# Nine weight slots instead of six in the expert loops of a hybrid decoder, with another gather and another layout of the second weight

## The reference, cut to what matters

```python
def layer(x):
    x = layer_norm(ALPHA * x + mixer(x))          # attention, then GDN in layer 1
    return layer_norm(ALPHA * x + moe_ffn(x))

def expert_block(args):                           # xb: the tokens of expert e
    xb, e = args
    hb = jax.nn.silu(xb @ w1[e]) * (xb @ w3[e])   # w1, w3: 1024 x 512
    return hb @ w2[e]                             # w2: 512 x 1024
```

## Time and profile before

| what | value |
|---|---|
| times of 3 runs | 1581.01, 1584.68, 1586.67 us (median 1584.68) |
| profiled execution: time, span | 1582.79 us, 1581.0 us |
| busy PE, PE weight load, DVE, ScalarE | 76%, 56%, 29%, 17% of the span |
| TensorE clock granted, mean | 0.934 |
| DMA over the whole span | 461.77 MB, 292 GB/s, 63246 packets |
| expert weights | 192 DMAs of 2 MB, median 26.5 us from issue to landing |

### The profile page before, as it was taken

How to read it: one execution, slowest core, us unless ns; L and a number is a source line. 1 busy time by engine, 2 the same in 40 slices (tenths; PEclk the granted TensorE clock), 3 DMA queues, 4 the chain that set the end, 5 groups by cost and what they waited for, 6 DMA issues and landing times. The chain is left out here.

```text
span 1581.0 us, 40565 instructions
## 1 busy us (share of the span) xinstructions
PE 1202.8 (76%) x17935; PEld 891.0 (56%) x17935; DVE 457.4 (29%) x1369; ACT 274.8 (17%) x676; POOL 34.8 (2%) x42
## 2 busy tenths in 40 slices
PE   8999676666666666799989899997866666666664
PEld 4444464554554554588888887543655555455553
DVE  1344511111111111465656544313211111111113
ACT  1232200000000000235244346202000000000000
POOL 0000300000000000000000000002000000000000
PEclk9999799999999999899999999998899999999998
DMA  9620599999999999943300001405799999999995
GB/s 362 243 107 16 196 425 426 427 425 426 429 425 426 428 426 423 355 160 107 129 32 1 1 28 55 157 4 236 313 427 426 425 427 427 426 425 428 425 427 234
DMA packets 63246, 461.77 MB, mean 292 GB/s; under 512 B 3872, under 2 KB 4016, under 8 KB 30416
## 3 DMA queue, kind: packets, MB, share of 16 engines
q1 hardware_dynamic: 61680, 455.90, 70.2%
q0 software_dynamic: 1504, 5.00, 0.9%
HBM read 459.83 MB, written 1.05 MB: 292 GB/s over the span
## 5 line engine op out<-in xcount | busy, mean ns | idle before, releaser
L711 PE MATMUL bank<-ring,arena 128*32 128x128 f32 x8192 | 311.0, 311 | 282.8 <-DMA ring<-in_moe_w 280.1
L711 PEld LDWEIGHTS bank<-ring,arena 128*32 128x32 f32 x8192 | 268.9, 123 | 332.9 <-DMA ring<-in_moe_w 241.3
L1009 ACT ACTIVATE arena<-bank 128x512 f32<-128x512 f32 (+3 forms) x294 | 128.9, 456 | 342.0 <-PE bank L680 97.9
L1485 DVE SCALAR_TENSOR_TENSOR arena<-arena,bank 128x128 f32<-128x128 f32 x64 | 18.4, 288 | 503.8 <-ACT arena L1085 503.8
L1085 ACT ACTIVATE arena<-bank 128x128 f32<-128x128 f32 x64 | 17.8, 278 | 691.9 <-PE bank L711 691.9
L725 PE MATMUL bank<-ring,arena 128*32 128x256 f32 x2048 | 124.4, 382 | 5.2 <-DMA ring<-in_moe_w 3.5
L765 PE MATMUL bank<-xT,ring 128*128 128x256 f32 x512 | 115.6, 385 | 0.0
L765 PEld LDWEIGHTS bank<-xT,ring 128*128 128x128 f32 x512 | 98.5, 194 | 16.5 <-issue 3.3
L677 PEld LDWEIGHTS bank<-arena 128*128 128x128 bf16 x3072 | 89.8, 97 | 11.1 <-issue 10.3
L677 PE MATMUL bank<-arena 128*128 128x32 bf16 x3072 | 87.0, 177 | 10.1 <-DVEq L1459 8.3
L725 PEld LDWEIGHTS bank<-ring,arena 128*32 128x32 f32 x2048 | 63.8, 109 | 47.6 <-issue 14.4
(11 more groups left out here) (218 smaller groups left out, 1122.0 us busy)
## 6 DMA issues: line engine op xcount, KB each, us to landing
ring<-in_moe_w SPq DMA_DIRECT2D x192, 2048.0 KB, 26.5
ring<-in_gdn_w_in SPq DMA_DIRECT2D x12, 2048.0 KB, 14.9
ring<-in_ab_w_in SPq DMA_DIRECT2D x5, 2048.0 KB, 24.0
ring<-in_gdn_w_out SPq DMA_DIRECT2D x4, 2048.0 KB, 8.0
ring<-in_ab_w_out SPq DMA_DIRECT2D x2, 2048.0 KB, 19.9
ring<-in_ab_w_in SPq DMA_DIRECT2D x2, 1024.0 KB, 8.6
x<-in_x SPq DMA_DIRECT2D x2, 512.0 KB, 4.9
arena<-in_mix_ln_g POOLq DMA_DIRECT2D x2, 512.0 KB, 5.4
```

What stands on the lines that cost most here:

```text
L711: last = mm(psum[5][h * CAP:(h + 1) * CAP, m * FH:(m + 1) * FH], xeT[:, j], ring[:, slots[m], j, h // 2 * SEQ + h % 2:(h // 2 + 1) * SEQ:2 ...
L1009: return do(o, i, ACT.Copy, **kw)
```

## The change

- Three more slots: `SLOTS = 9`, six in `ring` and three (`spare`) in `arena` from 24 to 72 KB, used by the experts alone. Attention and GDN keep to the ring. `MOE_SLOTS` orders them: layer 0 fills ring slots 0 to 5 and then the spares, layer 1 slots 4, 5, 0 to 3 and then the spares. The first nine units have waits of their own (`free_for_moe0`, `free_for_moe1`); a later unit waits for the expert three before it.
- PE's loop body and SP's hold six experts (`GROUP = 6`); five passes, two experts behind it.
- w2 is loaded as `(p c) n`, one run of 16 KB per partition, and the up projections read their weight at a stride of four (`h::TILES`).
- The gather: `pick` (now float32) is the stationary operand and x itself the moving one, 8 matmuls of 256 columns read at a stride of eight, in four column tiles. The result has tokens on partitions; ScalarE copies it (`xe`), PE transposes it (`turn_tokens`, two transposes), ScalarE copies it again (`xeT`). `parts`, `xs` and `res` go.
- Everything the experts use is packed into `arena` below 16 KB; `lnp` lies at 16 KB, for the GDN's norm at 48; `vtk`, `wba`, `ab` move.
- `transpose_x` fills a bank with one token tile, and DVE copies the last of the four banks. The router takes each token tile by itself, in four column tiles, summed by a matmul with a new constant `stack`.
- `route` leaves the shifted copies of `pos`, the repeats of `gate` and two memsets to other places; the count in `flag` comes after the first `picks`, and no engine waits for it before the experts.
- The GDN's output projection uses banks 4 to 7.

```diff
-OWN_HEAD, OWN_STEP, OWN_LAST = 7, 7, 2
+OWN_HEAD, OWN_MORE, OWN_STEP, OWN_LAST = 7, 20, 7, 2
@@
 RING = 6
+SLOTS = 9
+DEPTH = SLOTS // 3
+GROUP = 6
+GDN_OUT = 4
+MOE_SLOTS = ((0, 1, 2, 3, 4, 5, 6, 7, 8), (4, 5, 0, 1, 2, 3, 6, 7, 8))
@@
-        lnp = area(48, [2, D])
+        lnp = area(16, [2, D])
+        lnp_gdn = area(48, [2, D])
...
+        spare = [area(24 + 16 * i, [DJ, HALF]) for i in range(SLOTS - RING)]
+        def slot_tile(i):
+            return ring[:, i] if i < RING else spare[i - RING]
@@ expert_parts
-            w2 = a["moe_w2"][layer, bass.ds(e, 1)].rearrange("a (h p c) n -> (a p) h (c n)", h=2, c=2)
+            w2 = a["moe_w2"][layer, bass.ds(e, 1)].rearrange("a (p c) n -> (a p) (c n)", c=TILES)
@@ sync: load_experts
-                with sp.Fori(1, NE // 2) as i:
-                    for b in range(2):
-                        for m, src in enumerate(expert_parts(layer, i * 2 + b)):
-                            u = u0 + 3 * b + m
-                            sp.wait_ge((s.w1_used, s.h_ps, s.y_ps)[m], i * 2 + (b - 1 + s.e))
-                            sp.dma_start(part(m, u % RING), src).then_inc(slot_full[u % RING], 16)
+                def freed(n):
+                    def wait(m):
+                        sp.wait_ge((s.w1_used, s.h_ps, s.y_ps)[m], n + (s.e + 1 - DEPTH))
+                    return wait
+                for n in range(DEPTH):
+                    load_expert(n, n, lambda m: first_free(3 * n + m))
+                for n in range(DEPTH, GROUP):
+                    load_expert(n, n, freed(n))
+                with sp.Fori(1, NE // GROUP) as i:
+                    for c in range(GROUP):
+                        load_expert(i * GROUP + c, c, freed(i * GROUP + c))
@@
+            def free_for_moe0(u):
+                if u < 4:
+                    sp.wait_ge(proj_ps, 2 * (u + 2) + 2)
+                else:
+                    sp.wait_ge(mix_ps, 4)
+            def free_for_moe1(u):
+                if u < 2:
+                    sp.wait_ge(z_ps, 2 * u + 6)
+                elif u < 7:
+                    sp.wait_ge(mix_ps, 12)
+                else:
+                    sp.wait_ge(x_ready, 6)
@@ gpsimd
-            def parts(layer):
...
-            parts(0)
-            parts(1)
@@ tensor: router
-                for j in range(DJ):
-                    pe.wait_ge(xT_sb, 4 * (1 + 2 * layer) + j // 2 + 1)
-                    last = mm(psum[4][0:NE, 0:SEQ], rw[:, j], xT[:, j], start=(j == 0), stop=(j == DJ - 1))
+                for t in range(NT):
+                    transpose_x(n, t)
...
+                        last = mm(psum[5 + 2 * t][q * NE:(q + 1) * NE, 0:P], rw[:, j], xT[:, j, t * P:(t + 1) * P],
+                                  start=(j < TILES), stop=(j >= TILES), tile_position=(0, q * NE))
@@ tensor: gather
-                for j in range(DJ):
-                    for t in range(NT):
-                        for part in range(3):
-                            mm(psum[4][:, j * CAP:(j + 1) * CAP], xs[:, t, part, j], pick[:, b, t],
-                               start=(t == 0 and part == 0), stop=(t == NT - 1 and part == 2))
+                for t in range(NT):
+                    by_j = x[:, t].rearrange("p (q j) -> p j q", j=DJ)
+                    for h in range(TILES):
+                        mm(psum[4][h * CAP:(h + 1) * CAP, 0:Q].rearrange("p (c q) -> p c q", c=2), pick[:, b, t],
+                           by_j[:, h::TILES], start=(t == 0), stop=(t == NT - 1), tile_position=(0, h * CAP))
...
+            def turn_tokens(s, wait):
+                pe.wait_ge(s.xe, wait)
+                for c in range(2):
+                    last = transpose(psum[4][:, Q + c * P:Q + (c + 1) * P], xe[:, c], ident)
+                last.then_inc(s.hT_ps, 1)
@@ tensor: turn
-                                              ring[:, slots[m], j, h // 2 * SEQ + h % 2:(h // 2 + 1) * SEQ:2],
+                                              slot_tile(slots[m])[:, j, h::TILES],
...
+                        if not ends_here:
+                            turn_tokens(s, i * (2 * group) + (2 * c + 3 + 2 * s.e))
@@
-                with pe.Fori(0, steps // 2 - 1) as i:
-                    turn(i, False)
-                turn(steps // 2 - 1, True)
+                whole = (steps - 1) // group
+                with pe.Fori(0, whole) as i:
+                    turn(i, range(group), False)
+                turn(whole, range(steps - whole * group), True)
@@ vector: route
-                for q in range(PASSES):
-                    own(v.tensor_scalar(out=pos[:, :, q * NE:(q + 1) * NE], in0=t32, scalar1=-1.0 - q * CAP,
-                                        scalar2=None, op0=ALU.add))
-                dve.wait_ge(init, 1)
-                v.tensor_copy(flag[:, layer, 0:1], cnt).then_inc(flag_sb, 1)
+                own.link(v.tensor_scalar(out=pos[:, :, 0:NE], in0=t32, scalar1=-1.0, scalar2=None, op0=ALU.add))
```

More of the change, by code:

```diff
@@ L78, with slot_att, slot_gdn, slot_moe @@
 RING = 6
-UNIT_ATT = 0
-UNIT_MOE0 = UNIT_ATT + 8
-UNIT_GDN = UNIT_MOE0 + 3 * NE
-UNIT_MOE1 = UNIT_GDN + 16
+SLOTS = 9
+DEPTH = SLOTS // 3
+GROUP = 6
+GDN_OUT = 4
+def slot_att(u):
+    return (u + 4) % RING
+def slot_gdn(u):
+    return u % RING
+MOE_SLOTS = ((0, 1, 2, 3, 4, 5, 6, 7, 8), (4, 5, 0, 1, 2, 3, 6, 7, 8))
+def slot_moe(layer, u):
+    return MOE_SLOTS[layer][u % SLOTS]
+def fill_counts():
+    n = [0] * SLOTS
+    att, gdn, moe = [], [], []
+    def fill(slot):
+        n[slot] += 1
+        return n[slot]
+    for u in range(8):
+        att.append(fill(slot_att(u)) if u else 0)
+    for layer in range(2):
+        moe.append(list(n))
+        for u in range(3 * NE):
+            fill(slot_moe(layer, u))
+        if layer == 0:
+            for u in range(16):
+                gdn.append(fill(slot_gdn(u)))
+    return att, gdn, moe
+ATT_FILL, GDN_FILL, MOE_BASE = fill_counts()
 COLS = {}
@@ L693, in scatter, with experts, turn @@
                 return last
-            def experts(s, fulls, steps, first):
-                def turn(i, ends):
-                    for b in range(2):
-                        n = i * 2 + b
-                        slots = [(first + 3 * b + m) % RING for m in range(3)]
-                        filled = [i * 16 + 16 * ((first + 3 * b + m) // RING + (1 if slots[m] or fulls is not slot_full else 0))
+            def experts(s, fulls, steps, slot_of, base, size):
+                group = 2 if size == RING else GROUP
+                def turn(i, cs, ends):
+                    for c in cs:
+                        n, b = i * group + c, c % 2
+                        ends_here = ends and c == cs[-1]
+                        slots = [slot_of(3 * c + m) for m in range(3)]
+                        filled = [i * (16 * 3 * group // size) + 16 * (base[slots[m]] + (3 * c + m) // size + 1)
                                   for m in range(3)]
-                        pe.wait_ge(s.xe, n + (1 + s.e))
+                        pe.wait_ge(s.xe, i * (2 * group) + (2 * c + 2 + 2 * s.e))
                         pe.wait_ge(s.gpt, n + (2 + s.g))
@@ L717, in turn @@
                         transpose(psum[6][:, 0:P], hm, ident).then_inc(s.hT_ps, 1)
-                        if not (ends and b):
+                        if not ends_here:
                             gather(s, 1 - b, n + 2)
@@ L751, in gdn @@
             def gdn():
-                transpose_x(2)
+                for t in range(NT):
+                    transpose_x(2, t)
                 def project(n):
@@ L1385, in route @@
                 own(v.memset(gsum, NEG))
+                own(v.memset(y_e, 0.0))
+                own(v.memset(gpT[:, 1], 0.0))
+                last_xT(1 + 2 * layer)
                 dve.wait_ge(sc_sb, layer + 1)
@@ L1464, in experts @@
                         o2(v.tensor_copy(y[:, :, h * Q:(h + 1) * Q], psum[h][:].rearrange("p (t q) -> p t q", t=NT)))
+                    for q in range(1, PASSES):
+                        o2(v.tensor_scalar(out=pos[:, :, q * NE:(q + 1) * NE], in0=pos[:, :, 0:NE],
+                                           scalar1=-1.0 * q * CAP, scalar2=None, op0=ALU.add))
+                    for t in range(NT):
+                        o2(v.tensor_copy(gate[:, t, NE:NIT].rearrange("p (q e) -> p q e", e=NE),
+                                         gate[:, t, 0:NE].unsqueeze(1).to_broadcast([P, PASSES - 1, NE])))
+                    o2(v.memset(y_e, 0.0))
+                    o2(v.memset(gpT[:, 1], 0.0))
                     o2.wait()
-                o2(v.memset(y_e, 0.0))
-                o2.link(v.memset(gpT[:, 1], 0.0))
                 dve.sem_inc(s.y, 1)
@@ L1470, in experts @@
                 picks(0, 0)
+                if not base:
+                    o2.link(v.tensor_reduce(out=cnt, in_=psum[6][:, 2 * NE:3 * NE], axis=AX, op=ALU.max))
+                    dve.wait_ge(init, 1)
+                    o2(v.tensor_copy(flag[:, layer, 0:1], cnt))
+                    o2.wait()
```

(6 more changed lines are left out.)

279 lines of the change are left out of this document (139 added, 140 removed).

## The result

| | before | after |
|---|---|---|
| median of 4 runs, us | 1584.13 (1581.01 to 1586.67) | 1620.19 (1617.79 to 1622.38) |
| ratio, 95% interval | | 1.0222 (1.0201 to 1.0243) |
| span of the profiled execution | 1581.0 | 1615.9 |
| layer 0: first and last up projection of an expert (start, end) | 187.24, 635.3 | 181.71, 664.7 |
| layer 1: the same | 1112.53, 1560.6 | 1133.67, 1596.1 |

The forecast was 1543. The layer 0 stage ends 29.4 us later than before; layer 1's takes 8.2 us more, counted from the GDN norm's transposes (1083.6 to 1560.6 before, 1110.9 to 1596.1 after).

A forecast was written before the change was run, and what follows sets the result against it. Expert stages were taken as bound by weight DMA at about 426 GB/s. From 1582.79 us, -19.8 - 10.5 - 12.2 + 2 + 0.5 = -40.0 gave 1543 us, range 1537 to 1558.

The forecast's parts named there:

- Steps 1 and 2: Expert stage starts: three more slots and an earlier first expert close the stream's holes, -19.8 us layer 0, -10.5 layer 1.
- step 3: Expert weight loads: w2 in 16 KB runs lands 0.19 us faster per expert, -12.2 us in all.
- 1.3 us for the slow start of a stream: Start of each expert stage: restart loss of a stream that had stood, counted as saved in each layer.
- rival A: w2 loads: the 0.19 us is not due to its runs, so 1555 us; chance 0.12.
- Step 6: Up projections and gather: strides of four and eight taken as free; +4 us kept for the range.
- step 5: PE's loop body of six experts: extra code fetches cost 2 us (bounds 0.4 and 3.4), stops hidden by nine slots.
- Step 4: PE per expert: 9.1 us against 14.6 for the weights, so hidden; +0.5 us for both layers' last experts.
- B: Loop code fetches: all ride on one DMA engine of sixteen, 0.62 us a packet, 1596 us; chance 0.06.
- C: Expert stages: PE becomes the bound if strides cost over double, or double at lower clock; 1630 us, chance 0.05.

The follow-up runs named there:

- a3: Changed kernel with PE's loop body cut from six experts to three (three list buffers), stride of four and 16 KB runs kept: 1563.15 us, ratio 0.9853.
- a3_perm: Changed kernel with a body of three experts, stride of four, and the gather reading a sorted copy of x: 1551.64 us, ratio 0.9779.
- a3_stride2: Changed kernel with a body of three experts, w2 in two 8 KB runs and up projections at stride two: 1554.56 us, ratio 0.9804.
- a_stride2: Changed kernel, body of six kept, with w2 back in two 8 KB runs and up projections at stride two: 1577.26 us, ratio 0.9937.

## Why the prediction was wrong, step by step

The forecast missed by 77 us. Taken in this order, the runs account for it so: 57.0 by the loop's length (after to a3), 11.5 by PE's own time (a3 to a3_perm), 7.8 by the runs of w2 (12.2 forecast, 4.4 found). That leaves 0.8, within the spread. In another order the shares are others, for the two failures feed each other: the loop's length costs 57.0 us with the stride of four and 22.7 with two, the strides, with the runs of 16 KB that go with them, cost 42.9 with a body of six and 8.6 with three.

**Steps 1 and 2 held.** SP and DVE of the changed kernel, at the start of layer 0's experts:

```profile
159.55 0.81 SPq L432 DMA_DIRECT2D ring<-in_moe_w  x2
160.40 2.38 SPq L432 DMA_DIRECT2D arena<-in_moe_w  x3
185.61 14.51 SPq L432 DMA_DIRECT2D ring<-in_moe_w  x4
```

```profile
169.98 0.24 DVE L1469 TENSOR_SCALAR arena<-arena 128x64 f32<-128x64 f32 x1 [2.42 <-ACT arena L1149]
...
170.85 0.23 DVE L1471 TENSOR_TENSOR arena<-arena,rbias 128x64 f32<-128x64 f32 x1
```

Five units are issued together where there were two. The two DVE operations take 0.24 and 0.23 us in place of 2.52 and 1.49, now that POOL does nothing beside them. The first up projection comes at 181.71, 5.5 us before the old 187.24, though in this execution attention ended 2 us later (the issues at 159.55 against 157.50). The tenth issue at 185.61 was called for 182.5 to 184.6: 1 us off, because it waits for the end of up projections that now take longer. The sizes held too, where nothing else stood in the way: in a3_stride2 the last up projection of layer 0 ends at 615.6 in place of 635.3, 19.7 us earlier (19.8 forecast), and the rest to the end of layer 1's (1529.6 for 1560.6) is 11.3 us shorter (10.5 forecast). The sum without step 3 is 1555, and the kernel took 1554.56. The 1.3 us for the slow start of a stream rested on no row.

**Step 3, mis-sized.** w2's 0.19 us was the difference of two landings, and most of it is not due to the runs: rival A was right for about two thirds, 0.12 of 0.19.

**Step 6 failed.** I took no cost for a stride of four, since two costs nothing and no row showed four. It costs double (7.57 against 3.87). The one row I leaned on said little: 194 ns was a transpose's load at a stride of eight and 140 a transpose's contiguous one, but contiguous loads of that shape in matmuls take 194 ns too, as in the GDN projections of the kernel before:

```profile
L765 PEld LDWEIGHTS bank<-xT,ring 128*128 128x128 f32 x512 | 98.5, 194 | 16.5 <-issue 3.3
```

The twofold price was in the bounds, and the number that I gave for it, 13.8 us an expert, was nearly right (14.14). What I concluded from it was wrong: "still under 14.6, only the tails pay". A bound that is 0.5 us under another has no room, and there were two things to fill it. One is the head start: nine slots bring the weights forward, PE starts its first expert no earlier than 180, and 32 x 14.15 us from there end at 633 (in a3, at 13.9 an expert, it is 628.1), while the last weight of layer 0 lands at 618.6 in a3_stride2. With a deeper buffer it is the total of PE's work that counts, not the rate beside the transfers' rate. The other was step 5.

**Step 5 failed by its size and by its cover, and it weighed most.** That the code might be fetched in every pass was seen (77 packets more were the bound above), and the count of near 130 in that case too (149 came). Its price was put at 3.4 us, with all engines sharing the bytes, and the stops were left at nothing: "the stops hide in the nine slots". They hid only behind PE's slack, which step 6 had spent: a_stride2, with the slack, pays 22.7 us for the code, the changed kernel 57.0. To be slower than before took both failures: a body of six with the stride of two takes 1577 us (a_stride2), a body of three with the stride of four 1563 (a3). But each alone was enough to miss the stated range, which ended at 1558.

**Step 4** had PE at 9.1 us; with the stride of two it is 10.3 (the gather costs 1 more than I took), and hidden as I said (a3_stride2).

**Rivals.** B was right in kind and too harsh in one thing: not one engine of sixteen lags but half of them, so a packet's time is spread over eight. And a packet costs its engine more than the 0.62 us taken, 1.06 and about 0.5 for the load beside it. Its chance of 0.06 was too low: the count of near 130 packets was in my own step 5, and I left its cost to a mean over sixteen engines. C was right that PE would become the bound, but put the point at a cost of more than double; the point lay below it.

## What to carry to other kernels

Count a loop body in instructions before unrolling it over more slots: the one that stays resident costs nothing in each pass, a longer one is fetched anew, and a third buffer for the short lists was all that it took to halve it. The price of a fetch is paid twice, as a stop of the engine and as time of the DMA engines that carry it (some 0.19 us for each packet here), and code written out pays the second as well. Where one engine comes within some per cent of the bound, add up its work from its first to its last instruction, stops included, rather than compare one step with one step. A stride has a price of the same kind: for a float32 moving operand two was nearly free and four doubled the time, which cost nothing where PE had 6 us of slack and up to 43 us where it had none.

## What the runs showed of the hardware that was not expected

- PE's code: a body of three experts (some 5 packets) stays, 47 packets in all; one of four (7.2 by count) is fetched again in nine of twelve later passes, one of six in all. The Trainium skill's "Runtime: NRT & Kernel Launch" (Instruction fetch mechanics) gives PE 128 KiB in blocks of 16 KiB, which is 8; the runs agree for a body of six, but a body of 7.2 was not safe either.
- A refetch at the start of a pass beside a full DMA stopped PE for 4.6 to 6.6 us, in many passes with a second stop of 2.8 to 5.3 us behind it.
- A code packet holds one DMA engine for 1.06 us, lengthens one load packet by about 0.5, and rides on eight of the sixteen engines. With 131 packets or more these eight end the stream of layer 1 some 10 us after the others (0.50 of share, 206 to 213 GB/s), in a loop or written out; with 47, the share falls only in the last 2 us.
- In a3_perm the granted clock is 1.00, the level of 2.4 GHz, from 185 to 600 us, with PE busy 380 of 415 us; in a3_stride2, with PE busy 321 of them and idle for 2 to 3 us before most weights, the mean is 0.93. The slower parts cost nothing that can be seen: PE waits for weights there anyway.
